# Norms by square root on token columns, chained norms, context keys first and fused minima in a three-block float32 network

## The reference

```python
def rms_norm(x, g, eps=1e-6):
    y = x * lax.rsqrt(jnp.mean(x * x, axis=-1, keepdims=True) + eps)
    return y * g
```

## Time and profile before

| | us |
|---|---|
| median of 3 runs | 3531.26 (3529.25 to 3533.41) |
| profiled execution | 3528.3 |
| its span, first to last instruction | 3526.5 |
| PE busy | 3227.3 |
| DVE busy | 1517.3 |
| ACT busy | 716.1 |

### The profile page before, as it was taken

One profiled execution on the slowest core, in us unless ns is written; L12 is line 12 of the kernel. 1 busy time (PEld: TensorE's weight loads), 2 busy tenths in 40 slices (PEclk: granted clock), 3 DMA queues, 4 the chain that ended last, 5 costly groups with the idle time before them and its releaser, 6 DMA issues. The chain is left out here.

```text
span 3526.5 us, 39640 instructions
## 1 busy us (share of the span) xinstructions
PE 3227.3 (92%) x16518; PEld 1851.5 (53%) x16518; DVE 1517.3 (43%) x2332; ACT 716.1 (20%) x1104; POOL 0.2 (0%) x4
## 2 busy tenths in 40 slices
PE   7999998798996979989898988899998999999997
PEld 3475654343444433323332322687555887878874
DVE  2553238611378332221212221545433757475652
ACT  2210222302107210000000001100521332231403
POOL 0000000000000000000000000000000000000000
PEclk9999999999998989999999999999999999999999
DMA  7301143124110079999999999122111111121210
GB/s 259 120 3 49 34 150 109 39 82 155 60 75 27 25 327 428 428 427 428 427 428 427 428 427 399 48 94 90 54 48 67 56 69 56 64 72 48 72 48 24
DMA packets 120306, 588.36 MB, mean 167 GB/s; under 512 B 8896, under 2 KB 11072, under 8 KB 95424
## 3 DMA queue, kind: packets, MB, share of 16 engines
q1 hardware_dynamic: 120128, 585.83, 41.6%
HBM read 583.72 MB, written 2.10 MB: 166 GB/s over the span
## 5 line engine op out<-in xcount | busy, mean ns | idle before, releaser
L456 PE MATMUL ps<-hT,weight_ring 128*128 128x512 f32 x1216 | 541.3, 602 | 21.5 <-ACT hT L595 8.8
L456 PE MATMUL ps<-work,weight_ring 128*128 128x512 f32 (+1 forms) x960 | 422.8, 589 | 18.2 <-PEq L2679 8.3
L456 PEld LDWEIGHTS ps<-hT,weight_ring 128*128 128x128 f32 x1216 | 231.5, 193 | 307.9 <-issue 303.8
L456 PEld LDWEIGHTS ps<-work,weight_ring 128*128 128x128 f32 x960 | 180.5, 193 | 213.8 <-issue 203.2
L2252 PE MATMUL ps<-weight_ring,work 128*64 128x512 f32 x944 | 214.3, 597 | 32.1 <-DMA weight_ring<-in_w_up 19.5
L328 DVE TENSOR_TENSOR work<-work,ps 128x512 f32<-128x512 f32 x196 | 134.7, 687 | 248.7 <-PE ps L443 244.0
L443 PE MATMUL ps<-weight_ring 128*128 128x256 f32 x896 | 202.7, 379 | 0.0
L2382 DVE SCALAR_TENSOR_TENSOR xT<-ps,mod,xT 128x512 f32<-128x512 f32 x128 | 96.1, 751 | 224.8 <-PE ps L2270 222.5
L443 PE MATMUL ps<-hT,weight_ring 128*128 128x256 f32 x704 | 166.1, 393 | 19.5 <-DVE hT L604 15.6
L443 PEld LDWEIGHTS ps<-weight_ring 128*128 128x128 f32 x896 | 169.7, 190 | 24.7 <-issue 1.9
L2252 PE MATMUL ps<-work 128*64 128x512 f32 x672 | 153.3, 598 | 14.9 <-DMA work<-in_w_up 13.5
(11 more groups left out here) (399 smaller groups left out, 4186.6 us busy)
## 6 DMA issues: line engine op xcount, KB each, us to landing
weight_ring<-in_w_gate SPq DMA_DIRECT2D x34, 2048.0 KB, 40.3
weight_ring<-in_w_down SPq DMA_DIRECT2D x28, 2048.0 KB, 40.2
work<-in_w_up SPq DMA_DIRECT2D x27, 2048.0 KB, 38.9
weight_ring<-in_w_up SPq DMA_DIRECT2D x25, 2048.0 KB, 38.2
work<-in_w_down SPq DMA_DIRECT2D x21, 2048.0 KB, 40.3
weight_ring<-in_w_in_odd SPq DMA_DIRECT2D x20, 2048.0 KB, 7.8
weight_ring<-in_w_in SPq DMA_DIRECT2D x17, 2048.0 KB, 9.1
work<-in_w_gate SPq DMA_DIRECT2D x15, 2048.0 KB, 40.3
```

What stands on the lines that cost most here:

```text
L456: ins = pe.matmul(bank[0:m, 0:f], w[:, k, where:where + m], src[:, k, 0:ntok], start=k == 0, stop=k == kt - 1)
```

## The change

It does eight things.

1. The norms' sums become columns of tokens: the squares of 128 tokens are the stationary operand, a column of ones the moving one, four products per feature tile. ACT takes one Sqrt over 128x4, with its table loaded ahead (`warm`); DVE takes the reciprocal and one Newton step (`invert`); PE spreads the four columns over partitions and tokens by a product with the identity (`spread`); the scale reads the root from PSUM.
2. Behind the experts `ChainedNorm` takes both norms from one pass of squares, with two moving columns (ones and the squared gain). The scale of `hT` uses both roots and gains; the stream's own scale (`scale_stream`) hangs beside tiles 8 to 15 of the even layer's projection. `banks` there is 6.
3. The first block's weight sums of the even and of the odd layer go from DVE to POOL.
4. In block 2 the weight block with the context's keys comes first, and its four context tiles run ahead of the norm's scale (`normed_from=4`); `vpad` is cleared only at its ends, beside.
5. `PairAttention` takes the biased scores and their minimum in one operation. In neighbourhood attention the minimum is written one column behind the scores, and a second reduction reads it with the context's part; the bias is kept with the other sign and scaled.
6. In `spread` the vector part of a turn hangs one tile earlier.
7. The router multiplies the logits by the root after they stand in token columns, and takes the constant part once.
8. `block2_gains` and `odd_bounds` hang beside projections; the slots of block 3's weight ring are shifted by two.

The diff, cut to its core:

```diff
-        self.slot_of = [i % RING if i < first else (i - first) % len(self.slots) if i < last else (i - last) % RING3
+        self.slot_of = [i % RING if i < first else (i - first) % len(self.slots) if i < last else (i - last + 2) % RING3
...
+        for p, at in ch.pool_summed.items():
+            if n == 1 and ch.sum_order[i] == ch.sum_order[p] + 1:
+                dve.wait_ge(ch.S["first_sums"].sem, 4 * at + 4)
         out, x, y, op = ((s1, a21, a22, ADD), (s2, s1, a11, SUB), (s3, a11, a21, SUB), (s4, a12, s2, SUB))[n]
-        v(dve.tensor_tensor(out, x, y, op), ch.S["weight_sums"])
+        v(dve.tensor_tensor(out, x, y, op), ch.S["first_sums" if i in ch.pool_summed else "weight_sums"])
...
+            if norm and not normed_from:
+                norm.spread(pe)
             tensor_beside.get(-1, nothing)(pe)
...
-                        if n == 0 and norm:
+                        if n == normed_from and norm:
...
+        if pool_first:
+            @block.gpsimd
+            def _(pool):
+                pool_first(Line(pool, ch.S["pool_step"]), pool)
+
         @block.vector
         def _(dve):
             v = Line(dve, ch.S["vector_step"])
             if vector_first:
                 vector_first(v, dve)
             if norm:
+                norm.invert(v, dve)
...
-            pe.matmul(self.bank, self.ch.m("ones"), self.sq[:, k % 4, :], start=k == 0,
-                      stop=k == self.kt - 1).then_inc(self.sums.sem, 1)
+            w = self.column(k)
+            c = w.shape[1]
+            for i in range(self.parts):
+                ins = pe.matmul(self.bank[:, c * i:c * (i + 1)], self.sq[:, k % 4, i * P:(i + 1) * P], w,
+                                start=k == 0 and i == 0, stop=k == self.kt - 1, skip_group_check=True)
+            ins.then_inc(self.sums.sem, 1)
...
-        inverse_root(a, act, self.rstd, self.bank, 1.0 / (P * self.kt), self.ch.eps[:, 0:1], self.rooted)
+        a(act.activation(self.st, self.bank[:, 0:self.parts], ACT.Sqrt, bias=self.ch.eps[:, 0:1],
+                         scale=1.0 / (P * self.kt)), self.rooted)
+
+    def invert(self, v, dve):
+        v.after(self.rooted, 1)
+        half = half_mean(self.ch, v, dve, self.bank[:, 0:self.parts], 1.0 / (P * self.kt))
+        refine(self.ch, v, dve, self.st, half, self.inverted)
+
+    def spread(self, pe):
+        pe.wait_ge(self.inverted.sem, self.inverted.at(1))
+        ins = spread_columns(self.ch, pe, self.bank, self.st)
+        ins.then_inc(self.spread_out.sem, 1)
+        self.spread_out.total += 1
...
+def warm_root(ch, a, act):
+    a(act.activation(ch.sm[:, 188:189], ch.eps[:, 3:4], ACT.Sqrt, bias=ch.eps[:, 2:3]))
+
+
+def half_mean(ch, v, dve, total, scale):
+
+    half = ch.sm[:, 180:180 + total.shape[1]]
+    v(dve.tensor_scalar(half, total, -0.5 * scale, -0.5e-6, MUL, ADD))
+    return half
+
+
+def refine(ch, v, dve, root, half, done=None):
+
+    t = ch.sm[:, 184:184 + root.shape[1]]
+    v(dve.reciprocal(root, root))
+    v(dve.tensor_tensor(t, root, root, MUL))
+    v(dve.tensor_tensor(t, t, half, MUL))
+    v(dve.scalar_tensor_tensor(root, t, 1.5, root, ADD, MUL), done)
+
+
+def spread_columns(ch, pe, bank, st):
+
+    for i in range(st.shape[1]):
+        ins = pe.matmul(bank[:, i * P:(i + 1) * P], st[:, i:i + 1].to_broadcast([P, P]), ch.m("ident"), start=True,
+                        stop=True)
+    return ins
...
+    def prepare(self, v, dve):
+        v(dve.memset(self.columns[:, :, 0], 1.0))
+        v(dve.tensor_tensor(self.both, self.g, self.g2, MUL))
+        v(dve.tensor_tensor(self.columns[:, :, 1], self.g, self.g, MUL), self.columns_ready)
+
+    def column(self, k):
+        return self.columns[:, self.order[k], :]
+
+    def root(self, a, act):
+        a.after(self.sums, self.kt)
+        both = self.bank[:, 0:2 * self.parts].rearrange("p (i c) -> p i c", c=2)
+        a(act.activation(self.st, both[:, :, 0], ACT.Sqrt, bias=self.ch.eps[:, 0:1], scale=1.0 / D), self.rooted)
+        a.after(self.second, 1)
+        a(act.activation(self.r2, self.t, ACT.Sqrt, bias=self.ch.eps[:, 0:1]), self.second_root)
+
+    def invert(self, v, dve):
+        both = self.bank[:, 0:2 * self.parts].rearrange("p (i c) -> p i c", c=2)
+        v.after(self.rooted, 1)
+        half = half_mean(self.ch, v, dve, both[:, :, 0], 1.0 / D)
+        refine(self.ch, v, dve, self.st, half)
+        v(dve.scalar_tensor_tensor(self.t, both[:, :, 1], 1.0 / D, self.st, MUL, MUL))
+        v(dve.tensor_tensor(self.t, self.t, self.st, MUL), self.second)
+        half = half_mean(self.ch, v, dve, self.t, 1.0)
+        v.after(self.second_root, 1)
+        refine(self.ch, v, dve, self.r2, half)
+        v(dve.tensor_tensor(self.r2, self.r2, self.st, MUL), self.inverted)
+
+    def spread(self, pe):
+        pe.wait_ge(self.inverted.sem, self.inverted.at(1))
+        spread_columns(self.ch, pe, self.both_rooms, self.r2).then_inc(self.spread_out.sem, 1)
+        spread_columns(self.ch, pe, self.first_room, self.st).then_inc(self.spread_out.sem, 1)
+        self.spread_out.total += 2
...
+    def scale(self, v, dve):
+        v.after(self.spread_out, 1)
+        for k in range(self.kt):
+            v(dve.scalar_tensor_tensor(self.dst[:, k, :], self.src[:, k, :], self.both[:, k:k + 1], self.both_rooms, MUL, MUL),
+              self.scaled)
+
+    def scale_stream(self, k):
+        def part(v, dve):
+            v.after(self.spread_out, 2)
+            v(dve.scalar_tensor_tensor(self.src[:, k, :], self.src[:, k, :], self.g[:, k:k + 1], self.first_room, MUL, MUL))
+        return part
...
-                    v(dve.scalar_tensor_tensor(self.S[2 * (i % 4) + a][:, 0:w], self.score_banks(a)[:, 0:w], -self.scale, b,
-                                               MUL, SUB), self.softened)
+                    S, n = self.S[2 * (i % 4) + a], u["cols"]
+                    least = S[:, n:n + 1] if u["plain"] else self.st[:, 2 * (i % 3) + a, 1:2]
+                    v(dve.tensor_tensor_reduce(S[:, 0:w], self.score_banks(a)[:, 0:w], b, -self.scale, 3e38, ADD, MIN, least),
+                      self.softened)
                 for a in range(2):
                     if u["plain"]:
                         v.after(self.plain_scaled, 2 * i + a + 1)
-                    v(dve.tensor_reduce(self.st[:, 2 * (i % 3) + a, 1:2], self.S[2 * (i % 4) + a][:, 0:u["cols"]], AXX, MIN),
-                      self.taken_max)
+                        v(dve.tensor_reduce(self.st[:, 2 * (i % 3) + a, 1:2], self.S[2 * (i % 4) + a][:, w:u["cols"] + 1], AXX,
+                                            MIN), self.taken_max)
...
-            beside.add(places[min(i, len(places) - 1)], self.tensor(i), self.scalar(i), self.vector(i))
+            where = places[min(i, len(places) - 1)]
+            beside.add(where, self.tensor(i), self.scalar(i))
+            beside.add(max(np.ceil(where) - 1, -1) if i < len(places) else where, vector=self.vector(i))
...
+    tensor[3] = seq(tensor[3], context.spread)
     scalar[1] = seq(scalar[1], context_squares)
-    scalar[2] = seq(scalar[2], context.root, context.add_shift)
+    scalar[2] = seq(scalar[2], context.root)
+    scalar[3] = seq(scalar[3], context.add_shift)
     project(ch, 4, tiles, banks=6, extra_sync=load, tensor_beside=tensor, scalar_beside=scalar,
-            vector_beside={2: context.scale})
+            vector_beside={-1: block2_gains(ch), 2: context.invert, 3: context.scale})
...
-    tiles = [(0, "T", j * P, ch.hT, T, copy_to(a_[:, j, :])) for j in range(4)]
-    with nc.Block() as block:
-        @block.vector
-        def _(dve):
-            Line(dve, ch.S["vector_step"])(dve.memset(vpad, 0.0))
+    tiles = [(0, "T", j * P, hcT, L, copy_to(k[:, j, T:T + L])) for j in range(4)]
+    tiles += [(1, "T", j * P, ch.hT, T, copy_to(a_[:, j, :])) for j in range(4)]
+
+    def clear_ends(v, dve):
+        v(dve.memset(vpad[:, :, 0:15], 0.0))
+        v(dve.memset(vpad[:, :, 15 + T:542], 0.0))
...
+        tiles.append((2, "T", j * P, ch.hT, T, (part_a, part_v)))
+    tiles += [(0, "T", j * P, ch.hT, T, copy_to(k[:, j, 0:T])) for j in range(4)]
+    tiles += [(3, "T", j * P, ch.hT, T, copy_to(q[:, j, :])) for j in range(4)]
     tiles += [(4, "N", s * P, ch.hT, T, copy_to(v[:, s, :])) for s in range(4)]
     tiles += [(4, "N", s * P, hcT, L, copy_to(v[:, 4 + s, :])) for s in range(2)]
-    project(ch, 5, tiles, vector_after=conv_taps(ch, vpad, y), norm=norm, extra_sync=load_tables)
+    project(ch, 5, tiles, vector_first=clear_ends, vector_after=conv_taps(ch, vpad, y), norm=norm, normed_from=4,
+            extra_sync=load_tables, tensor_beside={0: norm.spread})
...
-                          start=True, stop=False)
-                ins = pe.matmul(ps[:, 1, s * E_:(s + 1) * E_], ch.m("ones"), constant, start=False, stop=True)
-            ins.then_inc(logits.sem, 1)
-            for s in range(4):
```

(35 more changed lines are left out.)

137 lines of the change are left out of this document (64 added, 73 removed).

## The result

The changed kernel takes 3501.78 us (median of 4 runs, 3498.28 to 3510.39) against 3530.26 for the kernel before in the same comparison: a ratio of 0.9919, 95% interval 0.99 to 0.9938, 28.5 us faster. The forecast was 3479, with a range of 3465 to 3505. Its profiled execution took 3498.28 us for a span of 3496.5, 30.0 us less than the span of before.

What follows compares the result with a forecast made beforehand. PE, busy 92% of the span, was taken as the bound, with DVE binding neighbourhood attention. Terms 13 + 9.5 + 8 + 0.9 + 14.9 + 4.9 + 1.4 = 52.6 off 3531.3 gave 3479 us, range 3465 to 3505.

Steps and rivals of the forecast that it cites:

- narrow passes over 0.14 us: Sign of being wrong, in the norms' sums: narrow passes were expected at 0.09 to 0.11 us each.
- a stop of PE above 2 us: Sign of being wrong: a new PE stop this long in any of the places the forecast listed.
- Part 1: Sparse attention's stream: vector turns one bucket earlier, ahead of the eviction, remove PE's waits; 13 us, between 8 and 15.
- Part 2: Mixer: context tiles cover the norm's chain, then the taps on DVE bind; 9.5 us, ends 6 and 10.5.
- Part 3: Neighbourhood attention: fused scores and minima at 0.80 us relieve DVE; 10 us, of which 8 taken, ends 0 and 12.
- Part 4: Router: fewer half-clock passes and no turned roots, shifting the whole experts' stream behind it; 0.9 us, ends 0 and 1.5.
- Part 5: Behind the experts: one chain for both norms, weight sums on POOL, hT's scale earlier; 14.9 us, ends 11 and 15.5.
- third rival: POOL's additions slow DVE's scales behind the experts and before the odd layer: 3492, up to some 3500; chance 0.10.
- rival 1: Narrow passes are dear, through unhidden weight loads or a lowered clock: 13 to 33 us back, 3492 to 3512; chance 0.15.
- Part 6: Before the odd layer: bounds' blocks moved beside, weight sums to POOL, scale starts earlier; 4.9 us, ends 3 and 5.5.
- Part 7: The kernel's end: scale at 3515.6 in place of 3517.01; 1.4 us, ends 0 and 1.7.
- Part 8: The norms' sums in their new shape: 352 narrow passes at 0.107 us cost what the old sums did; nothing gained.

Runs made afterwards that it cites:

- exp_early: The changed kernel with a one-element Exp on ScalarE added behind the router's root; one execution, 3496.08 us.
- after_again: The changed kernel itself, unchanged, run again in the same rounds as a later combined kernel; 3500.29 us, ratio 0.9911 to the kernel before.
- pool_waits: The changed kernel, but GpSimd begins its weight sums only when the norm's Newton step is done; 3491.37 us, ratio 0.9896 to the kernel before.

## Why the prediction was right, and where it was off

The time lay in the range, 23 us above the forecast, and this is partly luck. Parts 5 and 6 came out far below their own ends (2.9 for 11 to 15.5, 1.3 for 3 to 5.5). The range still held them because it had been widened for rivals which, as they were priced, did not come. Two of the prediction's signs of being wrong did show: narrow passes over 0.14 us (0.21 at half clock), and a stop of PE above 2 us (3.32 ahead of the second tile behind the experts). By its parts:

**Part 1 (13)** is 12.2, and its cause is shown: undone, the waits came back. The number is a little better than the reckoning: the stretch with the moved turns gained 14.6 us, and the output projection behind them gave 2.4 back. **Part 2 (9.5)** is 9.1, with the taps as the new bound as worked out. Less than half of it, 4.3 us, hangs on the order of the context's keys.

**Part 3 (8)** is 4.2 us, measured against the kernel before. The price taken for the fused operation, 0.80, was right (0.69 + 0.08). The step that was off is "of which I take 8": taken back, the fusion was worth 6.3, with PE and ACT at 0.89 and 0.88 of the time behind it; what makes 4.2 of 6.3 is open but for a slower start (5.37 us for 3.67), worth at most 0.5. The Trainium skill (VectorE: DVE Perf Modes, "Two Vector instructions with no wait between them") has an operation that also writes its accumulator as two instructions, and the rows agree. The two together took 0.77 us, not the 0.9 that the prediction worked out beside it.

**Part 4 (0.9)** is 0.2. The step "the turned roots go" forgot what the root's table leaves behind: Ln and Exp had left Exp for the softmax, Sqrt does not, and its load of 1.28 us now stands ahead of the selection (from the router's first product to the last selection 24.5 us before, 23.8 now, 22.2 in exp_early). A second step failed too, "so this shifts all of it": with the load gone the last expert's copy came 0.7 us later and not 1.7 earlier. What takes the gain up in between is shown only as far as the lower clock in exp_early.

**Part 5 (14.9)** is 2.9, the mis-sized term of this prediction. Two steps failed. "Some twelve DVE operations on four columns at 0.23, 3.2 us" was right for each operation (0.16 to 0.18) and wrong for four of them, which waited 7.2 us in sum for GpSimd. The forecast's third rival had the mechanism but looked for it at the scales, where it excluded it rightly, and never asked which of the small operations read twice from SBUF. The second step is the neutral price of the narrow passes: at full clock they are nearly what was taken (0.11 for 0.107), but the clock came down during them, which rival 1 had named, and the sums took 3.0 us longer than before. These two leave 4.3 us of gain at the start of hT's scale. The second tile keeps it, starting 8.9 us behind the scale in both kernels (PE's longer wait there, 3.32 us for 1.56, only says that its first tile was done sooner, in 4.20 us for 6.47). But the clock is 0.50 from 2200 to 2202, and from this tile's start to the third's it takes 5.0 us in place of 3.5: 1.4 more lost. **Part 6 (4.9)** is 1.3 for the first of these reasons, 3.5 us for two operations. **Part 7 (1.4)** is 0.5; its spread ran at half clock, 2.07 us for eight passes.

**Part 8 (nothing).** Beside a projection a narrow sum costs 0.04 us more than a wide one (7.76 from one addition to the next in the even layer's output projection, 7.72 before), so "nothing" was right for 32 of the 40 sums. It left out the context's passes, which with the sum beside them make 40 narrow ones in a row; the tile behind them took 1.8 us more. The 0.09 and 0.20 us of the prediction are window counts, which take in passes from outside: by their starts the passes of the earlier trace rows, too, come every 0.11 us at full clock and every 0.21 at half. The Trainium skill (TensorE: Matmul & The Clock Gate, "Wait — 56ns, not 53.3ns?") has a least start-to-start of about 25 ns; that is not what binds these float32 passes, at 0.11 us.

The -1.7 in the even layer is within what this stage does from one profile to the next: 424.4 us here, 422.9 in after_again, 422.4 in pool_waits, against 422.7 before.

## What to carry to other kernels

Work given to GpSimd is not free for VectorE: in these runs a VectorE instruction that reads two operands from SBUF, however small, and comes while a GpSimd addition or copy runs, stands still until that ends. Look through the critical chain for such instructions, start GpSimd's work behind it, or keep one operand in PSUM. When a chain of norm steps is made of short operations, ask as well what ScalarE's lookup table and PE's clock will be at its end: the tile behind a longer wait of PE can run at half clock and take up part of the gain. And follow a gain to the stage's end: one at the router's selection was gone at the last expert.

## What the runs showed that was not expected

A four-column operation took 2.19 us, the length of another engine's instruction. PE's clock fell to 0.50 while PE was never idle, 4 us into a stretch of two-column passes, and also with 256-column passes among them; with the same sums as 512 moving columns against a two-column load it stayed at 1.00 (7.03 us). Behind 40 one-column passes in block 1 a tile of wide ones took 8.81 us for 7.03, though PE had not stood still. And the stretch ahead of the first edit, the same in all these kernels, took 610.1 to 623.3 us, a spread half as wide as the effect that was measured.
